# Gathering rows with one fp32 product in place of two fp32r products, and the freed 8 KB as a seventeenth weight cell, in a decoder layer with 64 experts

## What is computed

```python
t = rms_norm(x, norm_ffn_g)                        # 256 x 1024
scores = sigmoid(t @ w_router)                     # 256 x 64
choice = scores + router_bias
# 4 of 8 groups of experts by the sum of each group's best two, then the best 8 experts of those
w = scores of the chosen; w = w / (sum(w) + 1e-20) * 2.5
for e in range(64):
    hid = silu(t @ w_gate_e[e]) * (t @ w_up_e[e])  # 1024 -> 256
    routed += gates[:, e] * (hid @ w_down_e[e])    # 256 -> 1024
x = x + routed + shared_expert(t)
```

## Time and profile before

| | |
|---|---|
| Time before, median of 3 runs (lowest to highest) | 631.88 us (631.42 to 634.49) |
| The profiled execution: its time | 634.1 us |
| The profiled execution: its span | 632.3 us |
| TensorE busy (matmuls) | 570.5 us, 90% of the span |
| VectorE / ScalarE / GpSimd busy | 204.2 / 141.4 / 24.5 us |
| Mean DMA rate over the span | 357 GB/s, 226.05 MB |
| Mean granted TensorE clock | 0.971 of 2.4 GHz |

### The profile page before, as it was taken

How to read it: one execution, slowest core, us unless ns; L and a number is a source line. 1 busy time by engine, 2 the same in 40 slices (tenths; PEclk the granted TensorE clock), 3 DMA queues, 4 the chain that set the end, 5 groups by cost and what they waited for, 6 DMA issues and landing times.

```text
span 632.3 us, 10029 instructions
## 1 busy us (share of the span) xinstructions
PE 570.5 (90%) x4073; PEld 372.3 (59%) x4074; DVE 204.2 (32%) x512; ACT 141.4 (22%) x264; POOL 24.5 (4%) x82
## 2 busy tenths in 40 slices
PE   7999998999999987998799999899979998589764
PEld 6888774546666554664476655666635565356332
DVE  2346587777225220222122212222222222022102
ACT  5427247433111110111011101111111111011100
POOL 1003224000000000000000000000000000000000
PEclk9999999999999998998799999999999999799979
DMA  8974178823899999999999999999999999999981
GB/s 253 372 249 200 47 287 316 335 87 135 350 395 380 380 423 421 420 421 421 422 421 420 420 420 420 421 422 421 420 420 421 420 420 421 421 420 423 420 342 72
DMA packets 40840, 226.05 MB, mean 357 GB/s; under 512 B 4064, under 2 KB 11272, under 8 KB 15832
## 3 DMA queue, kind: packets, MB, share of 16 engines
q1 hardware_dynamic: 39688, 223.38, 87.0%
q0 software_dynamic: 528, 1.87, 1.1%
q10 hardware_dynamic: 576, 0.13, 0.1%
HBM read 224.32 MB, written 1.05 MB: 356 GB/s over the span
## 4 chain that ended last, share of the span: by engine, by line
PE 50%; SPq 24%; DMA 18%; ACT 3%; issue 2%; DVE 2%; DVEq 0%; ACTq 0%
SPq L356 22%; DMA cell_gu<-in_w_up_e 17%; PE ps L1593 14%; PE ps L1615 7%; PE ps L1346 7%; PE ps L1567 4%; PE ps L1467 4%; PE ps L1363 3%; PE ps L1623 3%; PE ps L1514 2%; SPq L448 2%; PE ps L1353 1%; DMA x_in<-in_x 1%; PE ps L1319 1%; PE ps L1426 1%
## 5 line engine op out<-in xcount | busy, mean ns | idle before, releaser
L1593 PE MATMUL ps<-cell_gu,xg 128*64 128x256 f32 (+2 forms) x2048 | 197.6, 405 | 37.3 <-DMA cell_gu<-in_w_up_e 26.1
L1593 PEld LDWEIGHTS ps<-cell_gu,xg 128*64 128x64 f32 (+2 forms) x2048 | 127.6, 133 | 114.4 <-issue 67.8
L1615 PE MATMUL ps<-cell_d,e_hT 128*64 128x512 f32 (+2 forms) x512 | 96.5, 611 | 6.0 <-issue 5.6
L1222 DVE TENSOR_TENSOR e_h<-e_sg,ps 128x256 f32<-128x256 f32 x26 | 16.1, 619 | 199.5 <-ACT e_sg L767 199.5
L1283 DVE SCALAR_TENSOR_TENSOR ylo<-ps,gslot,yhi 128x512 fp32r<-128x512 f32 x52 | 39.0, 750 | 124.7 <-ACT yhi L781 124.7
L1615 PEld LDWEIGHTS ps<-cell_d,e_hT 128*64 128x64 f32 (+2 forms) x512 | 29.0, 128 | 59.6 <-issue 59.3
L781 ACT ACTIVATE yhi<-ps,gslot 128x512 fp32r<-128x512 f32 x52 | 35.8, 688 | 123.4 <-PE ps L1615 123.4
L767 ACT ACTIVATE e_sg<-ps 128x256 f32<-128x256 f32 x26 | 10.0, 385 | 222.1 <-PE ps L1593 222.1
L1567 PE MATMUL ps<-pick,xhi 128*128 128x256 f32 x208 | 45.2, 299 | 1.1 <-DVE pick L1140 1.1
L1623 PE MATMUL ps<-yhi,S 128*128 128x512 f32 x104 | 43.2, 415 | 1.6 <-ACT yhi L781 1.6
L1567 PE MATMUL ps<-pick,xlo 128*128 128x256 f32 x208 | 41.9, 283 | 0.0
(11 more groups left out here) (329 smaller groups left out, 511.9 us busy)
## 6 DMA issues: line engine op xcount, KB each, us to landing
cell_gu<-in_w_gate_e SPq DMA_DIRECT2D x64, 1024.0 KB, 25.8
cell_gu<-in_w_up_e SPq DMA_DIRECT2D x64, 1024.0 KB, 26.7
cell_d<-in_w_down_e SPq DMA_DIRECT2D x64, 1024.0 KB, 26.4
wA<-in_w_in SPq DMA_DIRECT2D x4, 1024.0 KB, 9.8
wo<-in_w_out SPq DMA_DIRECT2D x1, 4096.0 KB, 13.2
wR<-in_w_in SPq DMA_DIRECT2D x3, 1024.0 KB, 16.8
wV<-in_w_in SPq DMA_DIRECT2D x1, 2048.0 KB, 15.6
w_kv<-in_w_mem_kv SPq DMA_DIRECT2D x1, 2048.0 KB, 19.2
```

The source lines that it names most:

```text
L1222: nc.vector.tensor_tensor(dst[:].rearrange("q k p -> q p k"), e_sg[:].rearrange("q (p k) -> q p k", k=KH), ps[:, U, DE:2 * DE].rearrange(" ...
L1593: last = mm(ps[side * w:(side + 1) * w, U, cols], rows(k, slice(side * w, (side + 1) * w)), cell_gu[i][:, k, :], start=k == 0, stop=k == K ...
L1615: last = mm(ps[side * w:(side + 1) * w, Y[half], :], e_hT[:, kk, side * w:(side + 1) * w], cell_d[n][:, kk, half * 512:(half + 1) * 512], ...
```

## The change

The split of the rows is dropped. The gather, in `gather_step` and in the loop for experts with more tokens than slots (`extra_pair`), multiplies `xn2` itself, in fp32, by the same one-hot matrices read as fp32: 8 products for each half gather instead of 16. `xn2` stays in its place. The 8 KB of `xhi` (at `o_R`) become a cell, number 16, which the load of up 5 gets; SyncE issues that load by hand behind down 4. All later loads move up by one in the list of freed cells.

```diff
-    CELLS = 16
+    CELLS = 17
...
-    cell_of = dict(zip(loads, [0, 1, 3, 6, 4, 7, 5, 8, 9, 2, 10, 12, 11, 13, 14, 15]))
+    cell_of = dict(zip(loads, [0, 1, 3, 6, 4, 7, 5, 8, 9, 2, 10, 12, 11, 13, 14, 15, 16]))
...
-    cell_at = [o_ring + 8 * KB * i for i in range(12)] + [o_A + 16 * KB, o_A + 24 * KB, o_R + 8 * KB, o_O + 8 * KB]
+    cell_at = [o_ring + 8 * KB * i for i in range(12)] + [o_A + 16 * KB, o_A + 24 * KB, o_R + 8 * KB, o_O + 8 * KB, o_R]
...
-    xhi = at("xhi", o_R, [P, NT, KD, P], F32R)
...
-    xlo = at("xlo", o_V + 8 * KB, [P, NT, KD, P], F32R)
...
             load_fixed("down", 4)
+            load_fixed("up", 5)
             sp.wait_ge(ssq_act, 6)
...
                     evac_x2T(0)
-                    nc.scalar.copy(xhi[:, 0], xn2[:, 0]).then_inc(split_act, 1)
...
             evac_x2T(1)
-            nc.scalar.copy(xhi[:, 1], xn2[:, 1]).then_inc(split_act, 1)
...
-            def low_part(t):
-
-                dve.wait_ge(split_act, t + 1)
-                dve.wait_ge(x2T_ps, 2 * t + 2)
-                nc.vector.tensor_tensor(xlo[:, t], xn2[:, t], xhi[:, t].bitcast(F32), ALU.subtract).then_inc(split_dve, 1)
-
-            low_part(0)
             second_norm(1)
...
             route(0)
-            low_part(1)
             route(1)
...
-                    for i, (part, t) in enumerate(((xhi, 0), (xhi, 1), (xlo, 0), (xlo, 1))):
-                        last = mm(o, part[:, t, k, :], pick[c % 2][:, t, :], start=i == 0, stop=i == 3)
+                    for t in range(NT):
+                        last = mm(o, xn2[:, t, k, :], pick[c % 2][:, t, :].bitcast(F32), start=t == 0, stop=t == NT - 1)
...
-            pe.wait_ge(split_dve, 2)
             pe.wait_ge(pick_dve, picks_built(0))
```

More of the change, by code:

```diff
@@ L263, in hybrid_decoder_layer @@
             rg_act, camax_dve, cap_dve, oca_ps, oca_dve, yrg_dve, ysq_act, wo_ps, x1_dve, x2T_ps, x2T_act,
-            x2T_dve, split_act, rt_ps, score_act, route_dve, count_ps, cnt_dve, s_gu_ps,
-            s_sg_act, s_h_dve, s_hT_ps, s_hT_dve, pick_dve, order_pool, perm_dve, perm_ps, ids_dve, gateT_ps, gateT_act, gatev_ps, split_dve, gather_ps, xg_act, xg_dve, gu_ps,
+            x2T_dve, rt_ps, score_act, route_dve, count_ps, cnt_dve, s_gu_ps,
+            s_sg_act, s_h_dve, s_hT_ps, s_hT_dve, pick_dve, order_pool, perm_dve, perm_ps, ids_dve, gateT_ps, gateT_act, gatev_ps, gather_ps, xg_act, xg_dve, gu_ps,
             sg_act, h_dve, hT_ps, hTs_dve, pt_ps, S_act, gslot_dve, y_ps, s_down_ps, yhi_act, ylo_dve,
@@ L275, in hybrid_decoder_layer @@
             wT_ps wT_act o_ps yT_dve lam_act lam_dve gelu_dve gelu_act rg_act camax_dve cap_dve oca_ps
-            oca_dve yrg_dve ysq_act wo_ps x1_dve x2T_ps x2T_act x2T_dve split_act rt_ps
+            oca_dve yrg_dve ysq_act wo_ps x1_dve x2T_ps x2T_act x2T_dve rt_ps
             score_act route_dve count_ps cnt_dve s_gu_ps s_sg_act s_h_dve s_hT_ps s_hT_dve
-            pick_dve order_pool perm_dve perm_ps ids_dve gateT_ps gateT_act gatev_ps split_dve gather_ps xg_act xg_dve gu_ps sg_act h_dve hT_ps hTs_dve pt_ps S_act gslot_dve y_ps s_down_ps
+            pick_dve order_pool perm_dve perm_ps ids_dve gateT_ps gateT_act gatev_ps gather_ps xg_act xg_dve gu_ps sg_act h_dve hT_ps hTs_dve pt_ps S_act gslot_dve y_ps s_down_ps
             yhi_act ylo_dve ov_pick_dve ov_gather_ps ov_xg_act ov_xg_dve ov_pt_ps ov_S_act
@@ L1632, in extra_pair @@
                 for k in range(KD):
-                    for j, (part, t) in enumerate(((xhi, 0), (xhi, 1), (xlo, 0), (xlo, 1))):
-                        last = mm(ps[:, Y[k // 4], k % 4 * P:(k % 4 + 1) * P], part[:, t, k, :], ov_pick[:, t, :],
-                                  start=j == 0, stop=j == 3)
+                    for t in range(NT):
+                        last = mm(ps[:, Y[k // 4], k % 4 * P:(k % 4 + 1) * P], xn2[:, t, k, :], ov_pick[:, t, :].bitcast(F32),
+                                  start=t == 0, stop=t == NT - 1)
                     if k % 4 == 3:
```

## The result

The changed kernel takes 636.02 us (median of 8 runs, 634.5 to 638.21) against 632.5 us of the kernel before in the same comparison (8 runs, 631.39 to 635.37). The ratio is 1.0053 with a 95% interval of 1.0031 to 1.0076: it is 0.5% slower, where 0.58% faster was forecast. The profiled execution has a span of 634.1 us.

What follows compares the result with a forecast made beforehand. The DMA stream, at 421 GB/s without pause after the release at 208 us, was taken as the bound; 2.49 us (cell) plus 1.2 us (gather) made 3.7 us off the 631.88 us median: 628.2 us, 0.58% less, range 627.0 to 630.9.

Steps and rivals of the forecast that it cites:

- The gather's products: Gather on TensorE: 8 fp32 products at 215.9 ns replace 16 fp32r at 119.2; 0.89 to 1.53 us gained before 208 us.
- The rule of the Trainium skill: Gather's matmul price: true fp32 is four passes by the book; set aside for a measured ratio of 1.8.
- The rival that the prediction gave 0.03: Gather: an fp32 product costs four fp32r ones, 477 ns; release 8.9 us later, 6.4 us slower, 638.3 us; chance 0.03.
- The cell: Load of up 5 moves into idle DMA time near 145 to 155 us, one load fewer after the last trough: minus 2.49 us.
- The bound: End of kernel: when TensorE frees cells at 208 us, plus bytes not yet issued at 421 GB/s, plus the tail.
- products-alone rival: After 216 us TensorE binds somewhere, so the cell gives nothing; only the gather's 1.2 us counts, 630.7 us; chance 0.14.
- The split: Before the first gather: two ScalarE casts (1.06 us each) and two VectorE subtractions (1.22 us each) go; worth nothing.
- The register reads: SyncE's four reads for the first group of four experts fall behind one load of the pair released at 164.46; cost nothing.
- the last trough: DMA's last trough was said to end with two loads issued at 208.28; from there the stream never pauses.
- clock rival: End of kernel: TensorE's clock rises later, last up products take 1.0 us more, 629.2 us; chance 0.19.

Runs made afterwards that it cites:

- early kernel: 17 cells; fp32 only in the first gather and three halves ahead of 208 us, fp32r without low parts in 21 later halves; 634.78 us, 1.0039 of before.
- late kernel: 17 cells; fp32r without low parts ahead of the release at 208 us, fp32 in the 21 later halves; 628.96 us, 0.9949 of the kernel before.
- one product of the rounded rows with 17 cells: 17 cells; gather with one fp32r product of rows rounded in place, low parts left out; 624.96 us, 0.989 of the kernel before.
- the cell with the repeated fp32r products: 17 cells; rows rounded to fp32r in place, second pair of products repeats the first, low parts left out; 629.34 us, 0.995 of the kernel before.
- bf16 with 17 and 16 cells: Gather with two bf16 products for each fp32 one, about 16 bits kept; 629.57 us (0.9942 of before) with 17 cells, 632.16 us (0.9995) with 16.

## Why the prediction was wrong

**The step that failed** is in "The gather's products": "it gives 128 products in 27.63 us, 215.9 ns each". The 128 are records. The code of that line (the mixer's first 8 units of 8 products) has 64, so the same row says 431.7 ns for a product. The fp32r rows do have one record for each product (24 records are three steps of 8), so a record of the one was compared with a record of the other, and the half gather was sized as 8 x 215.9 = 1.73 us where it is 3.45. The sign of the term turned with it: 0.9 to 1.5 us gained ahead of 208 us became 7.7 us lost. Counting the loop against the x in the row would have shown it without any run.

**The rule of the Trainium skill was set aside wrongly.** The Trainium skill (FP8 and Floating Point Precision, TensorE Precision Notes) gives four passes for true fp32. The measured ratio of one fp32 product to one fp32r product is 431 / 119.2 = 3.6. The trace agrees with that rule roughly, if an fp32r product is one pass; no run here shows the passes. The rival that the prediction gave 0.03 had the right mechanism and 638.3 us; measured were 636.0. Its products were sized at 477 ns and cost 431, so that the release came 7.7 us later and not 8.9. It also took the whole delay as lost, which it was not (below).

**What held.** The cell: up 5 goes out at 137.94 and fills an idle stretch, and its worth of 2.49 us was measured as 2.5 to 3.4 us. (Its data took 8.8 us to land, so it was in at 146.7 us and not by 143 as forecast; nothing waited for it.) The bound: the time follows the release at 208 us and not TensorE's work behind it, as the early and the late kernel show. The products-alone rival, in which the cell gives nothing, is refuted by the kernels with and without it. The split costs nothing: the first gather starts at 152.36 and started at 152.59, the same but for the 0.24 us by which all of the changed execution is early. The register reads that now stand within a pair of loads put SyncE's next issue to 170.31 us, behind one at 167.33, and opened no trough: DMA moves 410 GB/s or more in each microsecond from 167 to 180 us.

**One reading was off.** The prediction has the last trough end with the loads issued at 208.28, and no pause from there on. The stretches show this trough from 209 to 216 us, behind that issue. Bytes that the stream still fails to move behind the release count as well.

**Why less was lost than the release was late.** The release is 7.7 us later and the cell gives 2.5 to 3.4 back, which makes 4.3 to 5.2; the change lost 3.5 us. What DMA had moved by 225 us, when the stream is at full rate in every kernel, accounts for the difference. The stretch from 140 to 225 us, in this order: the kernel before, the changed kernel, the change without its cell, and one product of the rounded rows with 17 cells:

```profile
140.00:225.00 85.00, 83.49 (x662) 51.96 (x664) 37.21 (x139) 19.10 (x34) 0.00 (x0) 1.00 0.84 335
```

```profile
140.00:225.00 85.00, 83.48 (x575) 53.21 (x574) 32.55 (x129) 15.98 (x30) 0.00 (x0) 1.00 0.79 317
```

```profile
140.00:225.00 85.00, 83.48 (x575) 53.04 (x574) 32.59 (x129) 15.95 (x30) 0.00 (x0) 1.00 0.75 304
```

```profile
140.00:225.00 85.00, 83.14 (x702) 49.14 (x704) 36.41 (x139) 18.86 (x34) 0.00 (x0) 1.00 0.90 369
```

The changed kernel has moved 18 GB/s x 85 us = 1.5 MB less than the kernel before, which is 3.6 us at 421 GB/s; measured were 3.5. Without the cell it is 2.6 MB or 6.3 us, measured 6.1; with one product it is 2.9 MB more, or 6.9 us sooner, measured 7.0. (A rate is rounded to 1 GB/s, which is 0.2 us here.) The other traces have 349 (the cell with the repeated fp32r products), 350 (late), 352 and 339 GB/s (bf16 with 17 and 16 cells), which are 2.8, 3.0, 3.4 and 0.8 us gained where 3.2, 3.2, 3.7 and 0.3 were measured. The early kernel's 313 GB/s are 4.4 us lost for 2.5 measured, in the execution that took 1.7 us more than its median. The part of a late release that costs nothing is the time in which DMA still moves loads issued earlier, as these rows up to the release show, of the kernel before and of the change without its cell:

```profile
140.00:208.09 68.09, 66.58 (x440) 41.74 (x442) 32.61 (x128) 15.69 (x28) 0.00 (x0) 1.00 0.81 323
```

```profile
140.00:215.66 75.66, 74.14 (x440) 46.95 (x442) 31.23 (x127) 14.55 (x27) 0.00 (x0) 1.00 0.74 299
```

These are 22.0 and 22.6 MB: at its release, 7.6 us later, the second has moved 0.6 MB more of the same loads, 1.5 us of the stream. The 6.1 us that are left are what was measured.

**What stays open.** The clock rival can't be judged, since each kernel has one profiled execution: the last up products took 5.17 us in the changed kernel, 5.87 in the one before and 6.61 in the fastest of all, so their length did not set the order of the times.

## What to carry to other kernels

Before a duration is taken from a row, its count is checked against the loop in the code; an instruction that leaves two records has half its price in each. In a kernel whose tail is a stream at full rate, what matters is how many bytes are still to be moved when the stream last stops waiting for releases: work ahead of that moment costs its time, less what the stream can still move meanwhile (6.1 of 7.6 us here), and work behind it costs nothing as long as the engine has room. A buffer more is worth about one transfer at the stream's rate, if there is an idle stretch to fill it in.

## What the runs showed of the hardware

At the full granted clock (1.00 in these stretches), an fp32 product (128x128 weights, 256 columns) costs 431 ns and shows as two matmul records and two weight loads; one in fp32r costs 119 ns and one in bf16 113 ns, with one record each. The bf16 operands were both read with a step of two. The mean weight load of 128 columns took 97 ns in bf16, even with that step, and 190 ns in fp32 and in fp32r. In all nine traces the stream moved 421 GB/s from 225 to 600 us.
